# Squared key norms of a delta rule: from the diagonal of the key scores instead of products of squares with ones

## The reference, cut to what matters

```python
def l2norm(x):
    xf = x.astype(jnp.float32)
    return xf * lax.rsqrt(jnp.sum(xf * xf, axis=-1, keepdims=True) + 1e-6)

# gdn_mixer
qkv = jax.nn.silu(causal_conv(jnp.concatenate([q, k, v], axis=-1), conv_w))
q = l2norm(q.reshape(B, S, GDN_HEADS, GDN_DK)) * (GDN_DK ** -0.5)
k = l2norm(k.reshape(B, S, GDN_HEADS, GDN_DK))
...
# chunk_gated_delta_rule
kk = jnp.einsum('bhntd,bhnjd->bhntj', kc, kc)
L = jnp.where(strict, bc[..., :, None] * kk * decay, 0.0)
sol = lax.linalg.triangular_solve(L + jnp.eye(C, dtype=L.dtype), rhs, ...)
```

## Time and profile before

| | us |
|---|---|
| median of 3 runs | 1375.73 |
| lowest and highest run | 1370.8, 1376.44 |
| span of the profiled execution (first to last instruction) | 1369.2 |
| PE busy, PEld busy | 1345.0, 1265.4 |
| DVE, ACT, POOL busy | 1040.0, 750.9, 46.3 |

### The profile page before, as it was taken

How to read it: one execution, slowest core, us unless ns; L and a number is a source line. 1 busy time by engine, 2 the same in 40 slices (tenths; PEclk the granted TensorE clock), 3 DMA queues, 4 the chain that set the end, 5 groups by cost and what they waited for, 6 DMA issues and landing times. The chain is left out here.

```text
span 1369.2 us, 26498 instructions
## 1 busy us (share of the span) xinstructions
PE 1345.0 (98%) x10828; PEld 1265.4 (92%) x10828; DVE 1040.0 (76%) x1781; ACT 750.9 (55%) x1157; POOL 46.3 (3%) x48
## 2 busy tenths in 40 slices
PE   8999999999999999999999999999999999999998
PEld 8899999998999989899999999999989899888996
DVE  6999898677766666999897767766778746777565
ACT  6544656556444455544557545544558546576363
POOL 0000000000000000000000000000000110001100
PEclk9999999999999999999999999999999999999999
DMA  8565444564665465645364555555553324353231
GB/s 289 177 207 178 131 154 160 180 215 155 197 202 185 139 230 163 215 155 185 97 204 159 187 187 172 198 185 191 178 186 124 120 64 137 100 174 109 78 102 69
DMA packets 108992, 223.77 MB, mean 163 GB/s; under 512 B 6180, under 2 KB 17700, under 8 KB 108872
## 3 DMA queue, kind: packets, MB, share of 16 engines
q1 hardware_dynamic: 106736, 219.12, 48.2%
q10 hardware_dynamic: 2136, 2.96, 0.7%
HBM read 221.01 MB, written 1.06 MB: 162 GB/s over the span
## 5 line engine op out<-in xcount | busy, mean ns | idle before, releaser
L1755 DVE TENSOR_TENSOR wlo<-ring,whi 128x1024 fp32r<-128x1024 f32 (+3 forms) x430 | 498.1, 1180 | 182.7 <-ACT whi L1173 152.7
L1173 ACT ACTIVATE whi<-ring 128x1024 fp32r<-128x1024 f32 (+3 forms) x430 | 433.2, 1026 | 361.8 <-PE bank L499 228.7
L499 PE MATMUL bank<-hhi,whi 128*128 128x256 f32 x2016 | 278.8, 280 | 6.0 <-ACT sgb L1431 3.9
L508 PE MATMUL bank<-hhi,wlo 128*128 128x256 f32 x2016 | 280.3, 281 | 0.0
L499 PE MATMUL bank<-hlo,whi 128*128 128x256 f32 x2016 | 275.3, 278 | 0.0
L499 PEld LDWEIGHTS bank<-hhi,whi 128*128 128x128 f32 x2016 | 253.1, 189 | 9.5 <-ACT sgb L1431 4.3
L508 PEld LDWEIGHTS bank<-hhi,wlo 128*128 128x128 f32 x2016 | 252.6, 189 | 3.7 <-issue 2.6
L499 PEld LDWEIGHTS bank<-hlo,whi 128*128 128x128 f32 x2016 | 251.6, 189 | 0.0
L469 PE MATMUL bank<-w 64*64 64x64 f32 (+5 forms) x1376 | 101.7, 249 | 1.5 <-DMA w<-in_flip 0.9
L1935 DVE SCALAR_TENSOR_TENSOR w<-w,par 128x256 f32<-128x256 f32 x240 | 98.0, 478 | 0.0
L521 PE MATMUL bank<-whi,hhi 128*128 128x512 f32 (+2 forms) x256 | 96.6, 379 | 0.0
(11 more groups left out here) (309 smaller groups left out, 1535.5 us busy)
## 6 DMA issues: line engine op xcount, KB each, us to landing
ring<-in_w_in SPq DMA_DIRECT2D x100, 1024.0 KB, 5.1
ring<-in_w_ffn_down SPq DMA_DIRECT2D x22, 1024.0 KB, 5.1
ring<-in_w_ffn_gate SPq DMA_DIRECT2D x20, 1024.0 KB, 5.1
ring<-in_w_ffn_up SPq DMA_DIRECT2D x20, 1024.0 KB, 5.1
ring<-in_w_merge SPq DMA_DIRECT2D x8, 1024.0 KB, 5.1
ring<-in_w_out SPq DMA_DIRECT2D x8, 1024.0 KB, 5.0
ring<-in_w_oc SPq DMA_DIRECT2D x4, 1024.0 KB, 5.3
ring<-in_w_od SPq DMA_DIRECT2D x4, 1024.0 KB, 5.2
```

Of the source, the lines that this page charges most:

```text
L499: done = e.matmul(o, wh[:, k, cols(u)], s_[:, k0 + k, :], stop=False, skip_group_check=True, start=opens and k == 0 and s_ is sh and u % 2 ...
L508: done = e.matmul(o, wl[:, k, cols(u)], sh[:, k0 + k, :], start=False, stop=closes, skip_group_check=True)
L1173: e.activation(part_of(whi, j), part_raw(j), ACT.Copy).then_inc(*up("hi.a"))
L1755: e.tensor_tensor(part_of(wlo, j), part_raw(j), part_of(whi, j), ALU.subtract).then_inc(*up("lo.v"))
```

## The change

The squares of the keys on ScalarE and their products with ones on TensorE are left out. Instead VectorE, in step 0 of `delta` at place 17, multiplies each bank of key scores with the identity matrix (repeated for the four heads) into `kdiag`, and sums each row of 128, which leaves the diagonal in `ss`. It does so for each token block just ahead of its `scores_v`. The addition of 1e-6 reads `ss` instead of a bank. `kdiag` lies where `ksq` lay; the squares of the queries, which go to the same place, now wait for the diagonal's sums instead of for the keys' sums.

```diff
@@ -323,7 +323,8 @@
-        ksq, qsq, sqo = c4(bufJ[:, :]), c4(bufJ[:, :]), c4(bufI[:, :])
+        kdiag = bufJ[:, :].rearrange("p (t h s) -> p t h s", t=2, h=4)
+        qsq, sqo = c4(bufJ[:, :]), c4(bufI[:, :])
@@ -957,8 +958,6 @@
                 for tb in range(2):
                     scores_p("delta.p", l, tb, kc, "L")
-                yield 1
-                squares_p("delta.p", l, ksq, "kc")
                 yield 4
@@ -1576,8 +1575,7 @@
             def squares_a(name, l, src, dst, tag):
-                if tag == "qc":
-                    e.wait_ge(*at("kc", "sums", l))
+                e.wait_ge(*at("kdiag", l, 1))
@@ -1588,8 +1586,6 @@
             def delta_a(l):
-                yield 1
-                squares_a("delta.a", l, kc, ksq, "kc")
@@ -2414,12 +2410,17 @@
                 for tb in range(2):
+                    e.wait_ge(*at("L", "scores", l, tb))
+                    e.tensor_tensor(kdiag[:, tb], heads(bank("L", "scores", l, tb)[:, :]), bc(ident, [P, 4, P]),
+                                    ALU.mult).then_inc(*up(name))
+                    e.wait_ge(*now(name))
+                    e.tensor_reduce(ss[:, 0, tb], kdiag[:, tb], AX.X, ALU.add).then_inc(*up(name))
+                    put(name, "kdiag", l, tb)
                     e.wait_ge(*at("Dm", l, tb))
                     scores_v(name, l, tb, "L", LT, Dm)
                 yield 1
-                e.wait_ge(*at("kc", "sums", l))
-                e.tensor_scalar(tflat(ss[:, 0]), bank("kc", "sums", l)[:, 0:8], 1e-6, None, ALU.add).then_inc(*up(name))
-                leave(name, "kc", "sums", l)
+                e.wait_ge(*at("kdiag", l, 1))
+                e.tensor_scalar(tflat(ss[:, 0]), tflat(ss[:, 0]), 1e-6, None, ALU.add).then_inc(*up(name))
```

## The result

The changed kernel takes 1384.12 us (median of 4 runs, 1379.68 to 1384.87) against 1375.31 us. The ratio on record is 1.0059, 95% interval 1.0045 to 1.0072, which on 1372 us is 8.1 us slower; the two medians are 8.8 us apart. Forecast were 1382.2 us, +6.5. The span of the profiled execution went from 1369.2 to 1377.9 us. Each run also gives TensorE's mean granted clock: 0.993 on average over the four runs; 90 runs of the kernel before, taken beside the experiments, gave 0.997.

The account below looks back on a forecast made before the run. TensorE, busy for 98%, was taken to bound the kernel. Per layer -1.9 (removal) + 3.45 (idle) + 1.7 (clock) = +3.25 us, +6.5 for two, giving 1382.2 us; range 1374 to 1387.

Parts of the forecast that it names:

- Removal: On TensorE, eight products with a column of ones leave each layer: 1.9 us less per layer, 3.8 us for the kernel.
- rival A: The gain stays: TensorE never waits for ScalarE's chain and each layer is 1.9 us shorter, -3.8 us, 1371.9; chance 0.13.
- Added work: On VectorE, two multiplications with the identity and two reductions per layer make the queries' taps start 2.45 us late.
- Delay on the path: After VectorE's idle time takes part back, second taps, SiLU and ScalarE's gapless chain to the queries' squares are 1.9 us late.
- Stall: TensorE stands idle 3.45 us per layer for the queries' squares and goes on 1.55 us later than before.
- Clock: TensorE's granted clock falls behind the stall, adding 1.7 us per layer; bounds nothing and 3.4.
- rival C: Clearly slower: TensorE stays at the lower clock twice as long, 4.95 us per layer, +9.9 us, 1385.6; chance 0.17.
- The reason for the clock: Idle times of 1.98 and 1.96 us brought TensorE's clock down, 1.24 us did not, so 3.45 us would.
- the price of 1.7 us: Three groups of eight products from 167.29 us took 4.43 us against 2.73 at full clock: 1.7 us lost per fall.

Follow-up runs that it names:

- e2: Changed kernel without the diagonal (eight scores stand in for the keys' sums), so only the removal is left; ratio 0.9997 to the kernel before, -0.4 us.
- e5: Changed kernel without the diagonal, the products for the queries' sums with 64 columns of ones instead of one; ratio 0.9987 to the kernel before, -1.8 us.
- e3: Changed kernel plus 14 extra products of ones on TensorE just ahead of its wait for the queries' squares; ratio 1.0017 to the kernel before, +2.3 us.
- e1: Changed kernel with the diagonal's four instructions and the keys' norm moved behind the second taps of the queries; ratio 1.0018 to the kernel before, +2.5 us.
- e7: Changed kernel with the delta task's steps at other places of the plan (scores and diagonal at 20); ratio 0.9993 to the kernel before, -1.0 us.
- e9: Changed kernel with the delta task's steps moved and BT formed at place 27 instead of 32; ratio 0.9988 to the kernel before, -1.6 us.

## Why the prediction was right

The forecast was +6.5 us by a stall and a fall of the clock in each layer, and the measured +8.1 came that way. That the sum came so near has some luck in it: the stall was put too high (3.1 us for both layers, measured 2.5) and the clock too low (3.4, measured 5.1 to 5.8). Step by step:

- *Removal.* The 1.9 us per layer were right as a length of TensorE's work: with the removal TensorE comes to each wait about 2 us earlier. As a gain they were never there in full. The squares of the queries were ready 0.33 us before TensorE came for them in the old profile, so about half of the removal turned into waiting even without the diagonal (0.69 us of wait in e2 and e5, and a gain of 1.0 us per layer in e5). The prediction's condition for rival A, VectorE no later at all, was too weak: with 0.33 us of slack VectorE had to be some 1.5 us earlier for the whole gain, and in e2, where it was 0.5 us earlier, TensorE still stood for 0.69.
- *Added work.* 2.45 us forecast, 2.39 measured at the taps.
- *Delay on the path.* 1.9 forecast, 1.6 measured at the SiLU and at the squares. I subtracted the brackets of the earlier trace rows as they stood; where VectorE's idle time is filled, the next instruction starts 0.08 us ahead of the end of the one before (1054.54 against 1052.17 + 2.45), so it gives back a little more than the bracket.
- *Stall.* 3.45 forecast, 3.06 measured; 1.55 us of delay forecast, 1.27 measured. The time of e3 agrees: +2.3 us for both layers.
- *Clock.* The term that was too small: 3.4 us forecast for both layers, 5.1 in the profile, 5.6 by the mean clocks, 5.8 by the time of e3. The first layer had the single fall that was forecast, the second the double fall of rival C. The outcome is thus between the forecast and rival C, and its 0.59% lies just beyond the 0.5% within which I had put most of the chance (0.56).
- *The reason for the clock* was told too simply. I read from the earlier trace rows that waits of 2 us bring the clock down and 1.24 us do not. A wait of 0.69 us brought it down in e2, the one of 1.24 us did in five of fourteen profiles, and one of 1.97 us did not in the changed kernel's first block. The fall at 167 us, from which I took the price of 1.7 us, cost the old kernel nothing in the end; the price was right for the second block where nothing gives the time back. What follows the wait counts as well: the same 0.69 us with wider products behind them left the clock up (e5).

Left open: why a wait of 1.09 us brought the clock down in e1 while waits of 1.07 us left it at 1.00 in e7 (e1 has waits of 0.20 and 0.21 us and the thin products just ahead of it; no run widened them), and what keeps e9 at -1.6 us of the 3.8 that were removed. Its waits for L2354 are 2.1 us in all against 1.5 in the kernel before, which accounts for 0.6 us of it.

## What to carry to other kernels

Work taken off the engine that is busy for 98% of the time is a gain only if what it waits for next comes earlier too: read how early each of its inputs is at that place before counting the work as saved. Work moved to an engine with idle time costs nothing or everything, by whether it stands ahead of or behind what others wait for; here the same four instructions were worth +8.1, +2.5 or -1.6 us at three places (for the last, other steps of the task were moved too). And count a wait of the matrix engine by what its clock does behind it, over several runs, not by its length; then look whether a later wait swallows that loss.

## What the runs showed of the hardware

- Short waits can cost more by the clock than by themselves. In e2 two waits of 0.69 us, followed by products with one column, went with a mean clock of 0.9954 for 0.9971, some 2.3 us.
- The same wait at the same place lowers the clock in one execution and not in another (1.98 us in the kernel before: 0.64 over 3 us; 1.97 us in the changed one: 1.00). The first block is the same in all fourteen kernels and has two such waits of 1.95 to 1.98 us; the clock fell behind 15 of the 28. A single profile's clock is no forecast of another's: the kernel before ran at 0.995 to 1.000.
- A fall of the clock can cost nothing, where TensorE would soon have to wait anyway. In the same profiles, TensorE stood for another 0.9 us for ScalarE some 27 us after each of the 13 waits without a fall, and after none of the 15 with one. A mean clock counts such falls like any other.
- Products with 64 columns of ones took hardly more time than with one column, 1.97 against 1.92 us for sixteen records at full clock, with 1.86 us of weight loads in both. As a means against a fall of the clock they are only seen to work where the wait was short.
